# One maximum and one exponential over 768 keys in two attention stages

## The chip, the cores and the metric

The kernel runs on one core of a Trainium2 chip. Its time is the device time of one execution in microseconds (us). A core has TensorE (PE; its weight loads are shown as PEld), VectorE (DVE), ScalarE (ACT), GpSimd (POOL) and SyncE (SP); each works through its own queue of instructions, and they meet at semaphores. TensorE writes to PSUM, of which there are eight banks of 512 float32 columns for each of 128 partitions.

## The reference

The kernel computes a whole network on 512 tokens in float32: a first block (feed-forward, RWKV-7 time mix beside dilated attention, feed-forward), then two hybrid layers over the 512 tokens and 256 context tokens. Only the attention of the two hybrid layers matters here. Each layer has six heads of multi-head latent attention (mla, 96 channels for the scores) and six query heads of grouped-query attention (gqa, 64 channels):

```python
def block_attention(q, k, v):
    scale = D ** -0.5
    def one_block(qi):                       # 128 queries
        s = jnp.einsum('bqgrd,bkgd->bgrqk', qi, k).astype(jnp.float32) * scale
        p = jax.nn.softmax(s, axis=-1).astype(v.dtype)
        return jnp.einsum('bgrqk,bkgv->bqgrv', p, v)
...
    o_mla = block_attention(q_mla, jnp.concatenate([k_mla, k_mla_c], axis=1),
                            jnp.concatenate([v_mla, v_mla_c], axis=1))
...
    if last:
        return x_new, ctx
    oc_mla = block_attention(mla_query(pc, mla_q_norm, mla_w_uq, None, None), k_mla_c, v_mla_c)
```

A block of token queries looks at all 768 keys (512 tokens and 256 context). In the first of the two layers the two blocks of context queries look at the 256 context keys alone; the second layer has no such blocks.

## The kernel before

The program is a chain of stages: feed-forward, time mix, dilated attention, feed-forward, then for each hybrid layer a norm, input products, gates, small products, the heads, and the output product. Weights stream in through two slots: SyncE loads a block, ScalarE rounds it, GpSimd forms the remainder, TensorE multiplies. In the heads stages there is nearly no such traffic.

The heads stage of a layer is a loop over pairs `j`. A pair is one block of 128 queries for two heads at once (`a` = 0 and 1, called units `u = 2j + a`). For three groups of heads the loop goes through the query blocks of mla and then of gqa: four wide pairs (768 keys) and, in the first layer, two narrow ones (256 keys) each. A pair goes through these steps:

- TensorE, `scores(j)`: query times keys into `SCORES[a]`, which is a pair of neighbouring PSUM banks for each unit; columns 0 to 511 are the token keys (the part `l`), 512 to 767 the context keys (the part `h`). For mla (L2387) a unit has one matmul over 512 and one over 256 columns, unit 0 first. For gqa (L2393) there are three of 256 columns, and the two units alternate. In the records of the profile each float32 matmul stands twice.
- VectorE, `largest(u)`: the maximum along the keys (L2497), part by part as the scores come, and the scaling of the larger one to a bias (L2500; L2502 for narrow pairs).
- ScalarE, `exponent(u)`: the exponential (L2463) of each part from PSUM to `PX`, with its sum along the keys, which is read out by an instruction of its own behind each.
- TensorE, `turned(j)`: 128x128 transposes of the exponentials (L2410), four for the part `l` and two for `h`.
- ScalarE copies the turned part `l` out of PSUM (L2478), VectorE the part `h` (L2516). VectorE also adds the sums of the two parts (L2507) and inverts them (L2510).
- TensorE, `values(j)`: the inverse sums spread over partitions (L2421) and the products with the values (L2425).
- VectorE, `result(j)`: two multiplications with the gate and the inverse sum (L2522, L2524); ScalarE and VectorE split the result in two for the next product (L2468, L2527).

The order on each engine is written out. TensorE goes `turned(j)`, `scores(j + 1)`, `values(j)`. VectorE takes the maxima and scalings of pair `j`, then the result of pair `j - 1`, then the copies and the inverse of pair `j`. ScalarE takes the exponentials of pair `j`, its copies, then the rounding of pair `j - 1`. There is one set of `SCORES`, so the scores of the next pair can only be written behind the exponentials of this one, which the transposes ahead of them on TensorE ensure. The function `heads_steps` lists the names that the engines count on their semaphores, in that order.

Of the kernel before, what the change touches and what calls it, by code (L numbers as in the profile page):

```python
# [26 lines left out]
ACT = mybir.ActivationFunctionType  # L27
ALU = mybir.AluOpType
AX = mybir.AxisListType.X
# [3 lines left out]
T = 512  # L33
TC = 256
TT = T + TC
# [22 lines left out]
BLOCKS = T // P  # L58
# [11 lines left out]
KB = TT // P  # L70
# [171 lines left out]
def block_kernel(nc, xT, ctxT, vec, square, first, levels, trig, lora, wstream, outT):  # L242
    nblocks = wstream.shape[0]
    with ExitStack() as ctx:
# [1582 lines left out]
        class Layer:  # L1827
# [81 lines left out]
            def heads_steps(self):  # L1909
                us = self.units()  # L1910
                n = len(us) // 2
                pe, act, dve = [], [], []
                def scored(j):
                    parts = ("l", "h") if us[2 * j][3] < BLOCKS else ("h",)
                    if us[2 * j][0] == "gqa":
                        return [f"sc{z}{2 * j + a}" for z in parts for a in range(2)]
                    return [f"sc{z}{2 * j + a}" for a in range(2) for z in parts]
                pe += scored(0) + [f"v{b}" for b in range(KB)]
                act += ["v0", "v1"]
                for j in range(n):  # L1920
                    low = us[2 * j][3] < BLOCKS
                    parts = ("l", "h") if low else ("h",)
                    both = (2 * j, 2 * j + 1)
                    pe += [f"tr{z}{u}" for u in both for z in parts] + (scored(j + 1) if j + 1 < n else []) + [f"pv{j}"]
                    act += [f"ex{z}{u}" for u in both for z in parts] + ([f"pt{u}" for u in both] if low else [])
                    act += [f"hi{j - 1}"] if j else []
                    for u in both:
                        dve += [f"mx{z}{u}" for z in parts] + [f"nm{u}"]
                    dve += [f"rg{j - 1}", f"y{j - 1}"] if j else [f"v{b}" for b in range(2, KB)]
                    dve += [f"pt{2 * j}"] + ([f"lo{j - 2}"] if j > 1 else []) + ([f"dn{j}"] if low else []) + [f"ri{j}", f"pt{2 * j + 1}"]  # L1930
                j = n - 1
                return pe, act + [f"hi{j}"], dve + [f"lo{j - 1}", f"rg{j}", f"y{j}", f"lo{j}"]

# [425 lines left out]
        def scale_of(kind):  # L2359
            return (MLA_NOPE + MLA_ROPE if kind == "mla" else HD) ** -0.5  # L2360

        COLS = 2 * KB
        SCORES, TURNED = two_banks[0:2], two_banks[2:4]
        VALUES = two_banks[3][:, TT:TT + 2 * P]

        def part_cols(u):
            return slice(u % COLS, u % COLS + 1), slice(COLS + u % COLS, COLS + u % COLS + 1)

        value_bank = lambda b: bank[4 + (b + 2) % 4]
        def head_values_out(b):  # L2370
# [2 lines left out]
        def heads_tensor(pe, L):  # L2373
# [4 lines left out]
            def scores(j):  # L2378
                kind, i, _, qb = us[2 * j]
                low = qb < BLOCKS  # L2380
                qs = slice(qb * P, (qb + 1) * P)
                pe.sem_inc(tensor_ready)
                if kind == "mla":
                    for a in range(2):
                        for z, at, w in (("l", 0, T), ("h", T, TC)):
                            if low or at:
                                pe.matmul(SCORES[a][:, at:at + w], QAM[:, i * 2 + a, qs], KAM[:, i * 2 + a, at:at + w], start=True, stop=True)\  # L2387
                                  .then_inc(*S.inc(f"sc{z}{2 * j + a}"))
                else:
                    for at in range(0 if low else T, TT, TC):  # L2390
                        for a in range(2):
                            hs = slice(a * HD, a * HD + HD)
                            mm = pe.matmul(SCORES[a][:, at:at + TC], QAG[hs, i, qs], KAG[hs, at:at + TC], start=True, stop=True)  # L2393
                            if at + TC in (T, TT):
                                mm.then_inc(*S.inc(f"sc{'l' if at < T else 'h'}{2 * j + a}"))
            def turned(j):
                low = us[2 * j][3] < BLOCKS
                for a in range(2):
                    u = 2 * j + a
                    for z, bs in (("l", range(BLOCKS)), ("h", range(BLOCKS, KB))):  # L2400
                        if z == "l" and not low:
                            continue
                        pe.wait_ge(*A.at(f"ex{z}{u}"))
                        if j == 0:
                            pe.wait_ge(*V.at("v5" if a else "v3"))
                        if j and a and z == "h":
                            pe.wait_ge(*V.at(f"y{j - 1}"))
                        pe.sem_inc(tensor_ready)
                        for b in bs:
                            mm = pe.transpose(TURNED[a][:, b * P:(b + 1) * P], PX[:, a, b * P:(b + 1) * P], eye)  # L2410
                        mm.then_inc(*S.inc(f"tr{z}{u}"))
# [36 lines left out]
        def heads_scalar(act, L):  # L2448
            st = L.heads
            A, V, S = st.act, st.dve, st.pe  # L2450
            us = L.units()
            n = len(us) // 2
            for b in range(2):
                act.wait_ge(*S.at(f"v{b}"))
                act.activation(*head_values_out(b), ACT.Copy).then_inc(*A.inc(f"v{b}"))
            def exponent(u):
                kind, _, a, qb = us[u]
                act.wait_ge(*V.at(f"nm{u}"))
                if u >= 2:
                    act.wait_ge(*S.at(f"trh{u - 2}"))  # L2460
                for z, c, cols in (("l", slice(0, T), part_cols(u)[0]), ("h", slice(T, TT), part_cols(u)[1])):
                    if z == "h" or qb < BLOCKS:
                        act.activation(PX[:, a, c], SCORES[a][:, c], ACT.Exp, scale=scale_of(kind), bias=NM2[:, u % COLS:u % COLS + 1],  # L2463
                                       accum_out=DEN2[:, cols]).then_inc(*A.inc(f"ex{z}{u}"))
            def rounded_part(j):
                kind, i, _, qb = us[2 * j]
                act.wait_ge(*V.at(f"y{j}"))
                act.activation(YHI[:, i + (0 if kind == "mla" else MLA_HEADS // 2), qb * P:(qb + 1) * P], YQ[:, j % 2, :], ACT.Copy)\  # L2468
                   .then_inc(*A.inc(f"hi{j}"))
            for j in range(n):  # L2470
                for a in range(2):
                    exponent(2 * j + a)
                if us[2 * j][3] < BLOCKS:
                    for a in range(2):
                        act.wait_ge(*S.at(f"trl{2 * j + a}"))
                        if j:
                            act.wait_ge(*S.at(f"pv{j - 1}"))
                        act.activation(PTS[:, a, 0:T], TURNED[a][:, 0:T], ACT.Copy).then_inc(*A.inc(f"pt{2 * j + a}"))  # L2478
                if j:
                    rounded_part(j - 1)  # L2480
                else:
                    round_block(act, L.out.b0 + 1)
            rounded_part(n - 1)

        def heads_vector(dve, L):
# [3 lines left out]
            n = len(us) // 2  # L2489
            def largest(u):  # L2490
                kind, i, a, qb = us[u]
                lo, hi = part_cols(u)
                nm = NM2[:, u % COLS:u % COLS + 1]
                for z, c, cols in (("l", slice(0, T), lo), ("h", slice(T, TT), hi)):
                    if z == "h" or qb < BLOCKS:
                        dve.wait_ge(*S.at(f"sc{z}{u}"))
                        dve.tensor_reduce(MX2[:, cols], SCORES[a][:, c], AX, ALU.max).then_inc(*V.inc(f"mx{z}{u}"))  # L2497
                dve.wait_ge(*V.at(f"mxh{u}"))
                if qb < BLOCKS:
                    dve.tensor_scalar(nm, MX2[:, lo], MX2[:, hi], -scale_of(kind), ALU.max, ALU.mult).then_inc(*V.inc(f"nm{u}"))  # L2500
                else:
                    dve.tensor_scalar(nm, MX2[:, hi], -scale_of(kind), None, ALU.mult).then_inc(*V.inc(f"nm{u}"))  # L2502
            def inverse(j):
                c, h = 2 * j % COLS, COLS + 2 * j % COLS
                dve.wait_ge(*A.at(f"exh{2 * j + 1}"))
                if us[2 * j][3] < BLOCKS:
                    dve.tensor_tensor(DEN2[:, c:c + 2], DEN2[:, c:c + 2], DEN2[:, h:h + 2], ALU.add).then_inc(*V.inc(f"dn{j}"))  # L2507
                    dve.wait_ge(*V.at(f"dn{j}"))
                    h = c
                dve.reciprocal(DEN2[:, c:c + 2], DEN2[:, h:h + 2]).then_inc(*V.inc(f"ri{j}"))  # L2510
            def high_part(u):
                j, a = u // 2, u % 2
                dve.wait_ge(*S.at(f"trh{u}"))
# [446 lines left out]
```

## Time and profile before

| | us |
|---|---|
| median of three runs (lowest, highest) | 2551.69 (2548.96, 2557.23) |
| span of the profiled execution, first to last instruction | 2548.6 |
| TensorE busy | 2434.8 (96%) |
| VectorE busy | 1208.9 (47%) |
| ScalarE busy | 1074.7 (42%) |
| GpSimd busy | 891.9 (35%) |

The page gives no time for the profiled execution other than its span. A matmul's end is modelled, so a busy TensorE need not be one at its peak. Shares over the whole span say little about a stage: the two heads stages lie at 1914 to 2090 us and 2351 to 2490 us. Useful views for them are the busy times in a window, the chain of waits in order of time, and the timeline of one pair.

### The profile page before, as it was taken

What the parts mean: (1) busy time and instruction counts of PE and PEld (TensorE: products, weight loads), DVE (VectorE), ACT (ScalarE), POOL (GpSimd) and SP (SyncE); (2) the same over time, 40 slices, a digit from 0 to 9 for tenths busy, and PEclk for the clock granted to TensorE, in tenths of its full rate; (3) what the DMA queues carried; (4) which work ended last, traced back from release to release, by engine and by line L of the source; (5) the groups of instructions that cost most, each with busy time, mean ns of one, the idle gap of its engine ahead of it and who ended that gap; (6) DMA issues with size and microseconds to landing.
All of it is one profiled execution on the core that took longest, in us unless ns stands there. A gap on an engine that the chain in (4) does not pass through costs nothing. (4 is left out here: it accounts for less than half of the span.)

```text
span 2548.6 us, 48956 instructions
## 1 busy us (share of the span) xinstructions
PE 2434.8 (96%) x18458; PEld 1982.8 (78%) x18458; DVE 1208.9 (47%) x2008; ACT 1074.7 (42%) x2172; POOL 891.9 (35%) x678
## 2 busy tenths in 40 slices
PE   8999999999999999999999999989999999898998
PEld 6888887878787887787888888878876678776776
DVE  3222225435363637454232222136777773567774
ACT  4333234444443434564343332243346652435662
POOL 3444453333334244224544444522320003233003
PEclk9999999999999999999999999989999999999999
DMA  4333332222223232112432333321110002122002
GB/s 145 97 92 99 102 107 93 68 91 62 91 66 93 60 98 75 59 50 77 140 101 91 99 99 99 100 65 50 58 50 26 2 1 66 42 74 76 17 2 75
DMA packets 52293, 188.44 MB, mean 74 GB/s; under 512 B 5792, under 2 KB 6048, under 8 KB 52000
## 3 DMA queue, kind: packets, MB, share of 16 engines
q1 hardware_dynamic: 50976, 181.74, 23.2%
q10 hardware_dynamic: 1152, 4.26, 0.5%
q8 instruction: 133, 2.18, 0.3%
q14 instruction: 32, 0.26, 0.0%
HBM read 183.88 MB, written 2.10 MB: 73 GB/s over the span
## 5 line engine op out<-in xcount | busy, mean ns | idle before, releaser
L2676 POOL TENSOR_TENSOR WLO<-RAW,WHI 128x512 fp32r<-128x512 f32 x668 | 886.1, 1348 | 1629.2 <-ACT WHI L318 1629.2
L318 ACT ACTIVATE WHI<-RAW 128x512 fp32r<-128x512 f32 x672 | 386.8, 623 | 972.1 <-PE psum L334 756.4
L332 PE MATMUL psum<-HHI,WHI 128*128 128x512 f32 x848 | 335.0, 395 | 14.1 <-POOL WLO L2671 8.7
L334 PE MATMUL psum<-HHI,WLO 128*128 128x512 f32 x848 | 331.1, 390 | 0.0
L333 PE MATMUL psum<-HLO,WHI 128*128 128x512 f32 x848 | 330.9, 390 | 0.0
L332 PE MATMUL psum<-H2HI,WHI 128*128 128x512 f32 (+1 forms) x536 | 196.8, 367 | 12.2 <-DVE H2LO L442 7.6
L332 PEld LDWEIGHTS psum<-HHI,WHI 128*128 128x128 f32 x848 | 159.8, 188 | 50.8 <-POOL WLO L2671 8.7
L333 PE MATMUL psum<-H2LO,WHI 128*128 128x512 f32 (+1 forms) x536 | 189.1, 353 | 0.0
L334 PE MATMUL psum<-H2HI,WLO 128*128 128x512 f32 (+1 forms) x536 | 188.9, 352 | 0.0
L333 PEld LDWEIGHTS psum<-HLO,WHI 128*128 128x128 f32 x848 | 159.9, 189 | 33.7 <-issue 1.2
L334 PEld LDWEIGHTS psum<-HHI,WLO 128*128 128x128 f32 x848 | 159.7, 188 | 33.6
L2463 ACT ACTIVATE PX<-psum,NM 128x512 f32<-128x512 f32 (+1 forms) x216 | 121.0, 565 | 93.6 <-DVE NM L2500 80.3
L332 PE MATMUL psum<-GHI,WHI 128*128 128x512 f32 x352 | 137.0, 389 | 0.9 <-DVE psum L666 0.9
L334 PE MATMUL psum<-GHI,WLO 128*128 128x512 f32 x352 | 136.9, 389 | 0.0
L333 PE MATMUL psum<-GLO,WHI 128*128 128x512 f32 x352 | 136.9, 389 | 0.0
L332 PEld LDWEIGHTS psum<-H2HI,WHI 128*128 128x128 f32 x536 | 102.6, 191 | 32.3 <-issue 8.2
L666 DVE TENSOR_TENSOR psum<-psum,FRSTD 128x512 f32<-128x512 f32 x44 | 30.8, 699 | 189.7 <-PE psum L334 189.6
L2497 DVE TENSOR_REDUCE MX<-psum 128x1 f32<-128x512 f32 (+1 forms) x216 | 108.0, 537 | 23.7 <-PE psum L2393 15.9
L333 PEld LDWEIGHTS psum<-H2LO,WHI 128*128 128x128 f32 x536 | 102.5, 191 | 16.2 <-issue 2.7
L334 PEld LDWEIGHTS psum<-H2HI,WLO 128*128 128x128 f32 x536 | 102.3, 191 | 14.0
L2410 PE MATMUL psum<-SQC,PX 128*128 128x128 f32 x624 | 89.0, 280 | 21.4 <-ACT PX L2463 14.4
L2410 PEld LDWEIGHTS psum<-SQC,PX 128*128 128x128 f32 x624 | 65.5, 141 | 43.4 <-issue 41.5
(416 smaller groups left out, 4835.5 us busy)
## 6 DMA issues: line engine op xcount, KB each, us to landing
RAW<-in_wstream SPq DMA_DIRECT2D x335, 512.0 KB, 3.6
X<-in_xT SPq DMA_DIRECT2D x8, 256.0 KB, 6.9
W3S<-in_lora ACTq DMA_DIRECT2D x5, 384.0 KB, 3.2
out_T<-OUT SPq DMA_DIRECT2D x3, 512.0 KB, 2.7
XC<-in_ctxT ACTq DMA_DIRECT2D x1, 1024.0 KB, 4.9
TRIG<-in_trig ACTq DMA_DIRECT2D x1, 960.0 KB, 8.0
FCC<-in_first SPq DMA_DIRECT2D x1, 576.0 KB, 8.7
RAW<-in_wstream SPq DMA_DIRECT2D x2, 256.0 KB, 3.8
```

The source lines that it names most:

```text
L318: act.activation(WHI[:, q % 2, half], RAW[:, q % 2, half], ACT.Copy).then_inc(rounded, 1)
L332: pe.matmul(out, tile_of(WHI, slot, u), hi(kt), start=first and last[0], stop=False)
L333: pe.matmul(out, tile_of(WHI, slot, u), lo(kt), start=False, stop=False)
L334: mm = pe.matmul(out, tile_of(WLO, slot, u), hi(kt), start=False, stop=end and last[1])
L666: dve.tensor_tensor(up, up, FRSTD[:, :], ALU.mult).then_inc(*st.dve.inc(f"up{n}"))
L2410: mm = pe.transpose(TURNED[a][:, b * P:(b + 1) * P], PX[:, a, b * P:(b + 1) * P], eye)
L2463: act.activation(PX[:, a, c], SCORES[a][:, c], ACT.Exp, scale=scale_of(kind), bias=NM2[:, u % COLS:u % COLS + 1], accum_out=DEN2[:, cols]) ...
L2497: dve.tensor_reduce(MX2[:, cols], SCORES[a][:, c], AX, ALU.max).then_inc(*V.inc(f"mx{z}{u}"))
L2676: pool.tensor_tensor(WLO[:, s, half], RAW[:, s, half], WHI[:, s, half].bitcast(F32), ALU.subtract).then_inc(split, 1)
```

## The change

A wide unit gets one maximum over its 768 columns and one exponential with one sum. TensorE signals `sc{u}` only when both parts of a unit's scores are written; VectorE waits for that, and the scaling has one operand to take from memory where it had two. The transposes of a unit wait for its one exponential. The addition of two partial sums is no longer there, and the small buffers of maxima and sums use one column for each unit, in a ring of 24 where it was 12. Narrow pairs keep their instructions.

```diff
-                        for z, at, w in (("l", 0, T), ("h", T, TC)):
+                        for at, w in ((0, T), (T, TC)):
                             if low or at:
-                                pe.matmul(SCORES[a][:, at:at + w], QAM[:, i * 2 + a, qs], KAM[:, i * 2 + a, at:at + w], start=True, stop=True)\
-                                  .then_inc(*S.inc(f"sc{z}{2 * j + a}"))
+                                mm = pe.matmul(SCORES[a][:, at:at + w], QAM[:, i * 2 + a, qs], KAM[:, i * 2 + a, at:at + w], start=True, stop=True)
+                        mm.then_inc(*S.inc(f"sc{2 * j + a}"))
...
-                            if at + TC in (T, TT):
-                                mm.then_inc(*S.inc(f"sc{'l' if at < T else 'h'}{2 * j + a}"))
+                            if at + TC == TT:
+                                mm.then_inc(*S.inc(f"sc{2 * j + a}"))
...
-                        pe.wait_ge(*A.at(f"ex{z}{u}"))
+                        if z == "l" or not low:
+                            pe.wait_ge(*A.at(f"ex{u}"))
...
-                for z, c, cols in (("l", slice(0, T), part_cols(u)[0]), ("h", slice(T, TT), part_cols(u)[1])):
-                    if z == "h" or qb < BLOCKS:
-                        act.activation(PX[:, a, c], SCORES[a][:, c], ACT.Exp, scale=scale_of(kind), bias=NM2[:, u % COLS:u % COLS + 1],
-                                       accum_out=DEN2[:, cols]).then_inc(*A.inc(f"ex{z}{u}"))
+                c = keys_at(qb)
+                act.activation(PX[:, a, c], SCORES[a][:, c], ACT.Exp, scale=scale_of(kind), bias=NM2[:, unit_col(u)],
+                               accum_out=DEN2[:, unit_col(u)]).then_inc(*A.inc(f"ex{u}"))
...
-                for z, c, cols in (("l", slice(0, T), lo), ("h", slice(T, TT), hi)):
-                    if z == "h" or qb < BLOCKS:
-                        dve.wait_ge(*S.at(f"sc{z}{u}"))
-                        dve.tensor_reduce(MX2[:, cols], SCORES[a][:, c], AX, ALU.max).then_inc(*V.inc(f"mx{z}{u}"))
-                dve.wait_ge(*V.at(f"mxh{u}"))
-                if qb < BLOCKS:
-                    dve.tensor_scalar(nm, MX2[:, lo], MX2[:, hi], -scale_of(kind), ALU.max, ALU.mult).then_inc(*V.inc(f"nm{u}"))
-                else:
-                    dve.tensor_scalar(nm, MX2[:, hi], -scale_of(kind), None, ALU.mult).then_inc(*V.inc(f"nm{u}"))
+                dve.wait_ge(*S.at(f"sc{u}"))
+                dve.tensor_reduce(MX2[:, unit_col(u)], SCORES[a][:, keys_at(qb)], AX, ALU.max).then_inc(*V.inc(f"mx{u}"))
+                dve.wait_ge(*V.at(f"mx{u}"))
+                dve.tensor_scalar(NM2[:, unit_col(u)], MX2[:, unit_col(u)], -scale_of(kind), None, ALU.mult).then_inc(*V.inc(f"nm{u}"))
...
-                if us[2 * j][3] < BLOCKS:
-                    dve.tensor_tensor(DEN2[:, c:c + 2], DEN2[:, c:c + 2], DEN2[:, h:h + 2], ALU.add).then_inc(*V.inc(f"dn{j}"))
-                    dve.wait_ge(*V.at(f"dn{j}"))
-                    h = c
-                dve.reciprocal(DEN2[:, c:c + 2], DEN2[:, h:h + 2]).then_inc(*V.inc(f"ri{j}"))
+                dve.reciprocal(DEN2[:, c:c + 2], DEN2[:, c:c + 2]).then_inc(*V.inc(f"ri{j}"))
```

On TensorE this is a wide gqa pair of the first hybrid layer before the change: the transposes of unit 0 and of unit 1, and the scores of the next pair behind them (`PX` holds the exponentials, `SQC` the identity).

```order
L2410 MATMUL psum<-SQC,PX 128x128 [waits scalar_steps]
L2410 MATMUL psum<-SQC,PX 128x128 x3
L2410 MATMUL psum<-SQC,PX 128x128 [waits scalar_steps]
L2410 MATMUL psum<-SQC,PX 128x128
L2410 MATMUL psum<-SQC,PX 128x128 [waits scalar_steps]
L2410 MATMUL psum<-SQC,PX 128x128 x3
L2410 MATMUL psum<-SQC,PX 128x128 [waits scalar_steps,vector_steps]
L2410 MATMUL psum<-SQC,PX 128x128
L2393 MATMUL psum<-KAG,QAG 128x256 x6
```

The same place after the change:

```order
L2408 MATMUL psum<-SQC,PX 128x128 [waits scalar_steps]
L2408 MATMUL psum<-SQC,PX 128x128 x5
L2408 MATMUL psum<-SQC,PX 128x128 [waits scalar_steps]
L2408 MATMUL psum<-SQC,PX 128x128 x3
L2408 MATMUL psum<-SQC,PX 128x128 [waits vector_steps]
L2408 MATMUL psum<-SQC,PX 128x128
L2390 MATMUL psum<-KAG,QAG 128x256 x6
```

TensorE waited for ScalarE four times and now waits twice, each time ahead of a unit's first transpose; number and order of its matmuls are as before.

On VectorE, the maxima (`MX_65`) and scalings (`NM_66`) of one wide pair, the previous pair's result and the inverse of the sums (`DEN_67`), before the change:

```order
L2497 TENSOR_REDUCE MX_65<-psum 128x1 [waits tensor_steps] x2
L2500 TENSOR_SCALAR NM_66<-MX_65 128x1 [waits vector_steps]
L2497 TENSOR_REDUCE MX_65<-psum 128x1 [waits tensor_steps] x2
L2500 TENSOR_SCALAR NM_66<-MX_65 128x1 [waits vector_steps]
L2522 TENSOR_TENSOR RG<-psum,GATES 128x128 [waits tensor_steps]
L2524 TENSOR_TENSOR YQ<-psum,RG 128x128 [waits vector_steps]
L2516 COPY PTS<-psum 128x256 [waits tensor_steps]
L2527 TENSOR_TENSOR YLO<-YQ,YHI 128x128 [waits scalar_steps]
L2507 TENSOR_TENSOR DEN_67<-DEN_67 128x2 [waits scalar_steps]
L2510 RECIPROCAL DEN_67<-DEN_67 128x2 [waits vector_steps]
```

And after it:

```order
L2490 TENSOR_REDUCE MX_65<-psum 128x1 [waits tensor_steps]
L2492 TENSOR_SCALAR NM_66<-MX_65 128x1 [waits vector_steps]
L2490 TENSOR_REDUCE MX_65<-psum 128x1 [waits tensor_steps]
L2492 TENSOR_SCALAR NM_66<-MX_65 128x1 [waits vector_steps]
L2508 TENSOR_TENSOR RG<-psum,GATES 128x128 [waits tensor_steps]
L2510 TENSOR_TENSOR YQ<-psum,RG 128x128 [waits vector_steps]
L2502 COPY PTS<-psum 128x256 [waits tensor_steps]
L2513 TENSOR_TENSOR YLO<-YQ,YHI 128x128 [waits scalar_steps]
L2496 RECIPROCAL DEN_67<-DEN_67 128x2 [waits scalar_steps]
```

Two maxima and the addition (L2507) are gone; the inverse waits for ScalarE itself.

## Rows read from the trace of the kernel before

**Rows 1.** Busy us (instructions) in the heads stages; then PEclk, DMA share, GB/s

```profile
core 0: us, PE busy (x) PEld busy (x) DVE busy (x) ACT busy (x) POOL busy (x), PEclk, DMA share, GB/s
1914.48:2090.18 175.70, 160.05 (x1458) 117.84 (x1458) 136.95 (x437) 110.12 (x331) 5.28 (x4) 1.00 0.03 7
2351.57:2489.84 138.27, 131.14 (x1219) 99.58 (x1219) 105.19 (x316) 93.71 (x271) 5.02 (x4) 1.00 0.04 13
```

**Rows 2.** Chain of waits, second heads stage: start us, us, what

```profile
2371.66 2.58 PE psum L2387 x8
...
2374.61 1.31 PE psum L2425 x24
2375.92 1.46 PE psum L2410 x12
2377.38 1.11 PE psum L2393 x8
2378.49 1.01 DVE MX L2497 x2
```

**Rows 3.** Timeline, a gqa pair: start us, us, engine, instructions [idle before, releaser]

```profile
1962.89 1.57 PE L2393 MATMUL psum<-KAG,QAG 64*128 64x256 f32 x12
...
1964.05 1.02 DVE L2497 TENSOR_REDUCE MX<-psum 128x1 f32<-128x512 f32 x2 [0.63 <-PE psum L2393]
...
1965.11 0.21 DVE L2500 TENSOR_SCALAR NM<-MX 128x1 f32<-128x1 f32 x1
1965.24 1.01 DVE L2497 TENSOR_REDUCE MX<-psum 128x1 f32<-128x512 f32 x2
1965.36 0.69 ACT L2463 ACTIVATE PX<-psum,NM 128x512 f32<-128x512 f32 x1 [1.78 <-DVE NM L2500]
...
1966.54 0.69 ACT L2463 ACTIVATE PX<-psum,NM 128x512 f32<-128x512 f32 x1
...
1967.46 0.86 PE L2410 MATMUL psum<-SQC,PX 128*128 128x128 f32 x6 [0.32 <-ACT PX L2463]
...
1968.25 0.70 PE L2393 MATMUL psum<-KAG,QAG 64*128 64x256 f32 x4
```

**Rows 4.** Timeline, an mla pair

```profile
2365.78 2.75 PE L2387 MATMUL psum<-KAM,QAM 128*128 128x512 f32 x8
...
2366.84 1.02 DVE L2497 TENSOR_REDUCE MX<-psum 128x1 f32<-128x512 f32 x2 [0.44 <-PE psum L2387]
...
2368.13 1.02 DVE L2497 TENSOR_REDUCE MX<-psum 128x1 f32<-128x512 f32 x2
...
2370.13 1.53 PE L2410 MATMUL psum<-SQC,PX 128*128 128x128 f32 x12
...
2371.50 2.75 PE L2387 MATMUL psum<-KAM,QAM 128*128 128x512 f32 x8
```

**Rows 5.** Groups by form, whole trace: xcount, busy us, mean ns, idle before

```profile
L2463 ACT ACTIVATE PX<-psum,NM 128x512 f32<-128x512 f32 x96 | 65.9, 687 | 81.6 <-DVE NM L2500 80.3
L2463 ACT ACTIVATE PX<-psum,NM 128x256 f32<-128x256 f32 x120 | 56.0, 467 | 12.0 <-DVE NM L2502 12.0
L2387 PE MATMUL psum<-KAM,QAM 128*128 128x512 f32 x96 | 49.2, 594 | 0.6 <-PE psum L334 0.6
L2310 ACT ACTIVATE YHI<-YC 128x768 fp32r<-128x768 f32 x2 | 1.7, 846 | 5.9 <-DVE YC L2346 5.9
L1706 DVE TENSOR_REDUCE MX<-psum 128x3 f32<-128x768 f32 x4 | 3.8, 948 | 0.0
```

**Rows 6.** One line's instructions: duration ns min/median/max, first and last start

```profile
L2502 DVE TENSOR_SCALAR NM<-MX x24: 153/154/154, 1941.3 to 2087.4; 128x1 f32<-128x1 f32 x24
```

**Rows 7.** Timeline, an mla pair that follows a narrow gqa pair

```profile
1976.98 1.02 DVE L2497 TENSOR_REDUCE MX<-psum 128x1 f32<-128x512 f32 x2
...
1979.21 0.86 PE L2410 MATMUL psum<-SQC,PX 128*128 128x128 f32 x6 [0.22 <-ACT PX L2463]
```

**Rows 8.** Timeline, the first pair of the first heads stage

```profile
1918.92 1.28 ACT L2463 ACT_TABLE_LOAD   x1
...
1922.26 0.87 PE L2410 MATMUL psum<-SQC,PX 128*128 128x128 f32 x6 [0.26 <-ACT PX L2463]
```

More of the change, by code:

```diff
@@ L1913, in scored @@
                 def scored(j):
[L1914 to L1917, printed above, removed]
+                    return [f"sc{2 * j + a}" for a in range(2)]
                 pe += scored(0) + [f"v{b}" for b in range(KB)]
@@ L1924, in heads_steps @@
                     pe += [f"tr{z}{u}" for u in both for z in parts] + (scored(j + 1) if j + 1 < n else []) + [f"pv{j}"]
-                    act += [f"ex{z}{u}" for u in both for z in parts] + ([f"pt{u}" for u in both] if low else [])
+                    act += [f"ex{u}" for u in both] + ([f"pt{u}" for u in both] if low else [])
                     act += [f"hi{j - 1}"] if j else []
                     for u in both:
-                        dve += [f"mx{z}{u}" for z in parts] + [f"nm{u}"]
+                        dve += [f"mx{u}", f"nm{u}"]
                     dve += [f"rg{j - 1}", f"y{j - 1}"] if j else [f"v{b}" for b in range(2, KB)]
-                    dve += [f"pt{2 * j}"] + ([f"lo{j - 2}"] if j > 1 else []) + ([f"dn{j}"] if low else []) + [f"ri{j}", f"pt{2 * j + 1}"]
+                    dve += [f"pt{2 * j}"] + ([f"lo{j - 2}"] if j > 1 else []) + [f"ri{j}", f"pt{2 * j + 1}"]
                 j = n - 1
@@ L2360, in scale_of @@
             return (MLA_NOPE + MLA_ROPE if kind == "mla" else HD) ** -0.5
-        COLS = 2 * KB
+        COLS = 4 * KB
         SCORES, TURNED = two_banks[0:2], two_banks[2:4]
         VALUES = two_banks[3][:, TT:TT + 2 * P]
-        def part_cols(u):
-            return slice(u % COLS, u % COLS + 1), slice(COLS + u % COLS, COLS + u % COLS + 1)
+        unit_col = lambda u: slice(u % COLS, u % COLS + 1)
+        keys_at = lambda qb: slice(0 if qb < BLOCKS else T, TT)
         value_bank = lambda b: bank[4 + (b + 2) % 4]
@@ L2491, in largest @@
                 kind, i, a, qb = us[u]
-                lo, hi = part_cols(u)
-                nm = NM2[:, u % COLS:u % COLS + 1]
-                for z, c, cols in (("l", slice(0, T), lo), ("h", slice(T, TT), hi)):
-                    if z == "h" or qb < BLOCKS:
-                        dve.wait_ge(*S.at(f"sc{z}{u}"))
-                        dve.tensor_reduce(MX2[:, cols], SCORES[a][:, c], AX, ALU.max).then_inc(*V.inc(f"mx{z}{u}"))
-                dve.wait_ge(*V.at(f"mxh{u}"))
-                if qb < BLOCKS:
-                    dve.tensor_scalar(nm, MX2[:, lo], MX2[:, hi], -scale_of(kind), ALU.max, ALU.mult).then_inc(*V.inc(f"nm{u}"))
-                else:
-                    dve.tensor_scalar(nm, MX2[:, hi], -scale_of(kind), None, ALU.mult).then_inc(*V.inc(f"nm{u}"))
-            def inverse(j):
-                c, h = 2 * j % COLS, COLS + 2 * j % COLS
-                dve.wait_ge(*A.at(f"exh{2 * j + 1}"))
-                if us[2 * j][3] < BLOCKS:
-                    dve.tensor_tensor(DEN2[:, c:c + 2], DEN2[:, c:c + 2], DEN2[:, h:h + 2], ALU.add).then_inc(*V.inc(f"dn{j}"))
-                    dve.wait_ge(*V.at(f"dn{j}"))
-                    h = c
-                dve.reciprocal(DEN2[:, c:c + 2], DEN2[:, h:h + 2]).then_inc(*V.inc(f"ri{j}"))
+                dve.wait_ge(*S.at(f"sc{u}"))
+                dve.tensor_reduce(MX2[:, unit_col(u)], SCORES[a][:, keys_at(qb)], AX, ALU.max).then_inc(*V.inc(f"mx{u}"))
+                dve.wait_ge(*V.at(f"mx{u}"))
+                dve.tensor_scalar(NM2[:, unit_col(u)], MX2[:, unit_col(u)], -scale_of(kind), None, ALU.mult).then_inc(*V.inc(f"nm{u}"))
+            def inverse(j):
+                c = 2 * j % COLS
+                dve.wait_ge(*A.at(f"ex{2 * j + 1}"))
+                dve.reciprocal(DEN2[:, c:c + 2], DEN2[:, c:c + 2]).then_inc(*V.inc(f"ri{j}"))
             def high_part(u):
```

## Prediction

> **What bounds the kernel now.** I first looked at where the change lives: the two stretches in which the attention heads run, 1914 to 2090 us and 2351 to 2490 us, 314 us together [rows 1]. In both TensorE is busy over 90% of the time and its granted clock is 1.00 throughout, while VectorE is busy 76 to 78% and ScalarE 63 to 68%. So nothing is simply full, and the next view is the chain of waits. It shows two regimes side by side [rows 2]. Up to 2377.38 it is TensorE alone: scores 2.58, values 1.31, transposes 1.46 us, one after the other. These are mla pairs. From 2377.38 it leaves TensorE: scores, then VectorE's two maxima (1.01 us), its scaling, ScalarE's exponential, and back to TensorE for six transposes (0.86 [rows 3]). These are gqa pairs. So the same four steps are hidden in one kind of pair and are the path in the other.
>
> The timeline gives both periods, counted from the first score matmul of a pair to that of the next: 5.37 us for gqa (1962.89 to 1968.25 [rows 3]) and 5.72 for mla (2365.78 to 2371.50 [rows 4]). Only pairs over all 768 keys are touched. Counts from the grouped rows [rows 5]: 96 matmul records of form 128x512 on the mla score line at four to a pair make 24 mla pairs, and the 96 exponentials over 512 at two to a pair make 48 wide pairs, so 24 are gqa. The 12 narrow pairs (256 keys) keep one maximum and one exponential, as they had.
>
> **One gqa pair, step by step.** [rows 3]
>
> 1. The maximum waits longer. Before, it starts once the first 512 columns of scores are there, 1.17 us after the scores begin (1962.89 to 1964.05). Now it waits for all 768. In mla, 1536 columns take 2.58 us [rows 2], so 256 columns cost 0.43. In gqa the twelve records take 1.57 us in all and the chain puts 1.11 on the eight ahead of the maximum [rows 2, 3]: 0.46 for the rest. I take 0.43, the rest of the difference being the modelled end of the last matmul: **+0.43**.
> 2. Maximum and scaling of the first unit. The two maxima take 1.01 us end to end. One maximum over 128x768 in the same memory appears elsewhere in this trace and takes 948 ns [rows 5]. The scaling with two pointer operands takes 0.21 and becomes the form with one, 0.15, which the narrow pairs already use [rows 6]. From start of the maximum to start of the exponential that is 1.31 before and 0.95 + 0.04 + 0.15 + 0.03 = 1.17 after, the 0.04 and 0.03 being the gaps that stand there now: **-0.14**.
> 3. From the first exponential to the second: 1.18 now (1965.36 to 1966.54), in which ScalarE runs without a pause. Afterwards ScalarE would be free after 0.90, but VectorE's second maximum starts 0.13 after the first scaling starts (1965.11 to 1965.24) and takes 0.95 + 0.04 + 0.15 + 0.03 more, so the second exponential follows the first by 0.13 + 1.17 - 0.15 - 0.03 = 1.12: **-0.06**. ScalarE's larger saving is not used: VectorE comes last.
> 4. From the second exponential to its transposes: now 0.92 (1966.54 to 1967.46), because TensorE turns the first 512 columns while ScalarE still works on the other 256. Then all six transposes wait for the whole row. An exponential over 512 takes 687 ns and over 256 takes 467 [rows 5], so 256 columns cost 220 and one over 768 about 907 (an estimate from these two rows): **+0.22**. The six transposes then take what they take now (0.79 to the next scores), since they already run back to back after the first part.
>
> Sum +0.45 us, a period of 5.82. Nothing covers it: the scores of the next pair stand behind these transposes on TensorE, and the maxima stand behind the scores. Times 24: **10.8 us**.
>
> **One mla pair.** [rows 4] Here TensorE's own work has to be overtaken before anything costs. With the same steps, the first maximum moves from 2366.84 to 2367.27. The second starts at 2368.13 now, on its scores; it moves to 2368.56, its exponential to 2368.56 + 0.95 + 0.04 + 0.15 + 0.03 = 2369.73, and its transposes become ready 0.92 + 0.22 later, at 2370.87. TensorE gets to them at 2370.13 plus half of the 1.46 us that twelve transposes take [rows 2], 2370.86. So the cover is used up almost exactly: 0 to 0.1. I take +0.10, since a wait that ends last leaves a small gap on TensorE. In 20 mla pairs: **2.0 us**. In two more, which follow a narrow gqa pair, TensorE has little to do in front: transposes start at 1979.21 now [rows 7]. The second maximum moves from 1976.98 to 1977.41, the transposes to 1977.41 + 1.17 + 1.14 = 1979.72: +0.5 each, **1.0 us**. In the first pair of each stretch a table load of 1.28 us ends at 1920.20, ahead of the first exponential, and the maxima have long been done [rows 8]; 1920.22 + 0.90 + 1.14 = 1922.26 is the time at which the second unit's transposes start now. Nothing.
>
> **Edits at nothing.** 48 additions of the two halves of the sum go, off the path: VectorE makes them after the second exponential while TensorE turns and scores. The wider column buffers cost no instruction. TensorE's and the DMA queues' instructions stay the same in number; no transfer is moved. Behind the longer wait of the maximum stand the scaling and the previous pair's result, whose inputs come later than that anyway. Behind the longer wait of the transposes stand the next scores, which is the cost counted above.
>
> **Sum.** 10.8 + 2.0 + 1.0 = 13.8 us on a span of 2548.6, the only time that the profile gives of its own execution. The three timed runs have a median of 2551.69 (2548.96 to 2557.23), 3.1 above that span, and I add to the median: **2565.5 us**, 0.54% slower.
>
> Bounds of what the trace does not show. The exponential over two banks at once: not under 0.85 (ScalarE's copy of 128x768 out of SBUF, 846 ns [rows 5]) and not over 687 + 467 = 1.15; that is -0.06 to +0.25 in every pair on the path, -1.4 to +11. I take 0.91, next to the lower end. The maximum over 768 into one column: 0.95 as the row has it, at most the 1.01 that two take now: up to +0.13 a pair, 6 us. The extra wait: 0 (the next 256 columns were there whenever the maximum started) to 0.46.
>
> The pages speak for the other sign. The Trainium skill, "Advanced Engine Details and Errata", section TRN2 Errata, The Read-Write Bubble, says that ScalarE and VectorE pay a memory latency between instructions and not inside one, advises large tiles, and says that one instruction may read several PSUM banks. The rows agree with the fixed part (467 - 220 = 247 ns of each exponential do not depend on its width). By that rule alone the merge is a gain, which is the third case below.
>
> **Rivals.**
>
> - *The mla pairs lose too.* For it: their cover is used up to within 0.1 us [rows 4], so any instruction longer than estimated is paid in all 22. With the merged exponential at 1.05 and the maximum at 1.0, each gqa pair pays 2 x 0.05 + 0.14 = 0.24 more and each mla pair, whose first maximum is not on the path, 0.19 more: 24 x 0.24 + 22 x 0.19 = 10 us more, 2575.5 us.
> - *The wait for the last 256 columns costs nothing.* If the score matmuls had all ended by the time the maximum starts, item 1 falls away and the gqa sum is +0.02, while the mla pairs stay covered: 2552 us, no change. Against it: in rows 3 the maximum starts at 1964.05 and the last score records run to 1964.46.
> - *The fixed costs decide (faster).* If ScalarE's queue sets the gqa period, each unit gives back 1.18 - 0.90 = 0.28 us, two units a pair, 24 pairs: 13.4 us, 2538 us. For it: ScalarE goes from the first unit's exponentials to the second's without a pause. It decides from the point at which the second scaling is done before ScalarE is free. Against it: VectorE needs 1.12 us a unit (item 3) where ScalarE will need 0.90, and the rule leaves out both the wait of item 1 and the overlap of item 4, which are not instructions.
>
> **How the numbers follow.** My forecast 0.62, its own range 2559 to 2573 (gqa between +0.3 and +0.65, mla between 0 and 0.2); mla loses too 0.18; wait costs nothing 0.14; fixed costs 0.06. A measurement of this kernel tells some 0.3% (7.7 us) from no change. Slower by more than that: 0.62 x 0.97 + 0.18 = 0.78; within: 0.16; faster: 0.06. The range for 8 in 10 leaves out the fast case and the outer part of the others: 2554 to 2577.
>
> **What would show it.** In the changed profile: the gap ahead of the maxima in a gqa pair grows from 0.63 to about 1.05 us; its period goes from 5.37 to about 5.8, with the six transposes of the second unit behind the end of the exponential; the maximum near 0.95 us and the exponential near 0.91; mla periods stay between 5.72 and 5.9; the granted clock stays 1.00 in both stretches. The prediction is wrong if gqa periods stay at 5.4 or fall, or if the merged instructions take as long as the two parts did.

## The result, and the profile after

The changed kernel takes a median of 2567.1 us (2557.69 to 2570.81, nine runs) against 2553.52 (2548.96 to 2557.49, nine runs) of the kernel before on the same chips: a ratio of 1.0049, 95% interval 1.0040 to 1.0059, or 12.5 us (10 to 15) slower; the two medians lie 13.6 us apart. The forecast was 13.8 us slower, 2565.5 us. One execution further below, of the kernel with the change in mla pairs alone, took 3063.62 us at a granted clock of 0.747; it is left out of that kernel's median and ratio.

The two heads stages answer to [rows 1]: busy us of each engine and number of instructions in each stretch, then the granted clock, DMA share and GB/s, in the changed kernel.

```profile
core 0: us, PE busy (x) PEld busy (x) DVE busy (x) ACT busy (x) POOL busy (x), PEclk, DMA share, GB/s
1918.82:2100.55 181.73, 160.21 (x1458) 118.22 (x1458) 126.82 (x365) 100.91 (x235) 5.29 (x4) 1.00 0.02 7
2365.21:2508.62 143.41, 131.36 (x1218) 99.95 (x1218) 95.13 (x244) 84.29 (x175) 5.01 (x4) 1.00 0.04 12
```

They take 325.1 us where they took 314.0: 11.2 us longer. VectorE and ScalarE are each busy some 20 us less in them, so the change does what it says, and TensorE does as much as before in a longer time. The timeline of a gqa pair shows where it waits; it answers to [rows 3].

```profile
1968.49 1.57 PE L2390 MATMUL psum<-KAG,QAG 64*128 64x256 f32 x12
...
1970.09 0.96 DVE L2490 TENSOR_REDUCE MX<-psum 128x1 f32<-128x768 f32 x1 [1.06 <-PE psum L2390]
...
1971.09 0.15 DVE L2492 TENSOR_SCALAR NM<-MX 128x1 f32<-128x1 f32 x1
1971.15 0.95 DVE L2490 TENSOR_REDUCE MX<-psum 128x1 f32<-128x768 f32 x1
1971.27 0.90 ACT L2460 ACTIVATE PX<-psum,NM 128x768 f32<-128x768 f32 x1 [2.09 <-DVE NM L2492]
...
1972.33 0.90 ACT L2460 ACTIVATE PX<-psum,NM 128x768 f32<-128x768 f32 x1
...
1973.46 0.84 PE L2408 MATMUL psum<-SQC,PX 128*128 128x128 f32 x6 [0.21 <-ACT PX L2460]
...
1974.23 0.49 PE L2390 MATMUL psum<-KAG,QAG 64*128 64x256 f32 x2
```

The period, scores to scores, is 5.74 us where it was 5.37. VectorE waits 1.06 us ahead of the maximum where it waited 0.63, and the six transposes of the second unit start 1.13 us behind its exponential where they started 0.92. The merged instructions, as groups by form (to [rows 5]; count, busy us and mean ns, then idle time before them):

```profile
L2490 DVE TENSOR_REDUCE MX<-psum 128x1 f32<-128x768 f32 x96 | 91.7, 955 | 47.6 <-PE psum L2390 25.5 <-PE psum L2384 18.9
L2460 ACT ACTIVATE PX<-psum,NM 128x768 f32<-128x768 f32 x96 | 86.5, 901 | 102.5 <-DVE NM L2492 101.0
```

The maximum takes 955 ns and the exponential 901, where 948 and 907 were expected. An mla pair, to [rows 4]:

```profile
2379.42 2.75 PE L2384 MATMUL psum<-KAM,QAM 128*128 128x512 f32 x8
...
2380.92 0.96 DVE L2490 TENSOR_REDUCE MX<-psum 128x1 f32<-128x768 f32 x1 [0.87 <-PE psum L2384]
...
2382.21 0.96 DVE L2490 TENSOR_REDUCE MX<-psum 128x1 f32<-128x768 f32 x1
...
2383.39 0.91 ACT L2460 ACTIVATE PX<-psum,NM 128x768 f32<-128x768 f32 x1 [0.30 <-DVE NM L2492]
...
2383.78 1.59 PE L2408 MATMUL psum<-SQC,PX 128*128 128x128 f32 x12
...
2385.21 0.60 PE L2384 MATMUL psum<-KAM,QAM 128*128 128x512 f32 x1
```

In the kernel before, the second unit's exponential of the pair in [rows 4] was:

```profile
2369.44 0.69 ACT L2463 ACTIVATE PX<-psum,NM 128x512 f32<-128x512 f32 x1
```

Counted from the first score matmul, the maxima come 0.44 us later (1.50 and 2.79 where it was 1.06 and 2.35) and the second exponential 0.31 us later (3.97 where it was 3.66). And yet the period is 5.78 to 5.79 where it was 5.72: the twelve transposes start when they did and take 1.59 us instead of 1.53, the small gap in their middle being what is left of the wait.

The span of this profile is 18.5 us longer, of which only 11.2 lie in the heads stages. The other 7.3 became a question for the experiments.

### The profile page after: what moved, and what is told of

Its sections match the earlier page's. It is cut to its first block and busy times, and to the rows that moved or that the text cites. A ratio compares the mean times of both kernels' runs of the same rounds, so it can differ in the third digit from the quotient of the medians.

```text
span 2567.1 us, 48620 instructions
## 1 busy us (share of the span) xinstructions
PE 2443.6 (95%) x18458; PEld 1991.7 (78%) x18458; DVE 1189.0 (46%) x1864; ACT 1056.4 (41%) x1980; POOL 891.4 (35%) x678
## 5 line engine op out<-in xcount | busy, mean ns | idle before, releaser
L332 PE MATMUL psum<-HHI,WHI 128*128 128x512 f32 x848 | 335.1, 395 | 13.8 <-POOL WLO L2657 9.8
L332 PE MATMUL psum<-H2HI,WHI 128*128 128x512 f32 (+1 forms) x536 | 200.0, 373 | 11.2 <-DVE H2LO L442 6.6
L2460 ACT ACTIVATE PX<-psum,NM 128x768 f32<-128x768 f32 (+1 forms) x120 | 97.8, 816 | 114.4 <-DVE NM L2492 112.9
L2490 DVE TENSOR_REDUCE MX<-psum 128x1 f32<-128x768 f32 (+1 forms) x120 | 101.8, 848 | 48.9 <-PE psum L2390 26.7
```

Of the source, the lines that this page charges most:

```text
L332: pe.matmul(out, tile_of(WHI, slot, u), hi(kt), start=first and last[0], stop=False)
L2490: dve.tensor_reduce(MX2[:, unit_col(u)], SCORES[a][:, keys_at(qb)], AX, ALU.max).then_inc(*V.inc(f"mx{u}"))
```

## The experiments

In what was expected of each run, quoted here, theory A is the prediction's: the maximum waits for the last 256 columns, the transposes for the whole exponential. Theory B lays the loss to the exponential alone. For the trace, a period is the time from the first score matmul of a pair to that of the next, and "the heads" are the two stretches from the first score matmul to the output product, 313.97 us in the kernel before.

Most kernels are the one before with two rules, which say for a wide unit (kind, group, 0 or 1, query block) whether it gets one maximum and one exponential:

```diff
+                parts = (("l", slice(0, T), lo), ("h", slice(T, TT), hi))
+                if qb < BLOCKS and ONE_MAX(us[u]):
+                    parts = (("h", slice(0, TT), hi),)
...
+                parts = (("l", slice(0, T), part_cols(u)[0]), ("h", slice(T, TT), part_cols(u)[1]))
+                if qb < BLOCKS and ONE_EXP(us[u]):
+                    parts = (("h", slice(0, TT), part_cols(u)[0]),)
...
-                        pe.wait_ge(*A.at(f"ex{z}{u}"))
+                        if not (low and z == "h" and ONE_EXP(us[u])):
+                            pe.wait_ge(*A.at(f"ex{'h' if ONE_EXP(us[u]) else z}{u}"))
```

**The maximum alone.**

```diff
+ONE_MAX = lambda unit: True
+ONE_EXP = lambda unit: False
```

> One maximum over 768 keys, the exponential still in two parts. Theory A (the gqa pair pays for a longer wait, and apart from that for the transposes that start behind the whole exponential): the first maximum of a gqa pair starts 0.43 us later and is 0.12 us shorter with its scaling, the second exponential follows the first after 1.18 us (ScalarE's two parts, not VectorE), transposes 0.92 us behind it: period 5.37 + 0.31 = 5.68. mla stays at 5.72 (second exponential 0.29 later, transposes ready at 2370.65 of the old trace, TensorE there at 2370.86). 24 x 0.31 + 2 x 0.3 = 8 us slower. Theory B (the loss is the exponential's alone, the wait for the scores is paid back by the shorter maximum): gqa 5.37, no change in time.

Measured: 2559.28 against 2552.73 us, ratio 1.0028 (1.0017 to 1.0040); heads 320.65, 6.7 longer. gqa period 5.62, mla 5.72, and 5.59 for the two mla pairs behind narrow gqa pairs. Theory B falls. A's 5.68 was 0.06 too long, and the timeline of the gqa pair says why:

```profile
1954.70 0.69 ACT L2472 ACTIVATE PX<-psum,NM 128x512 f32<-128x512 f32 x1 [2.09 <-DVE NM L2514]
...
1955.57 0.15 DVE L2514 TENSOR_SCALAR NM<-MX 128x1 f32<-128x1 f32 x1
...
1955.83 0.68 ACT L2472 ACTIVATE PX<-psum,NM 128x512 f32<-128x512 f32 x1
```

ScalarE's second unit starts 1.13 us behind the first and its bias has been ready for 0.1 us. So ScalarE needs 1.12 to 1.13 us for the two parts, and the 1.18 of the kernel before [rows 3] held a short wait for VectorE.

**The exponential alone.**

```diff
+ONE_MAX = lambda unit: False
+ONE_EXP = lambda unit: True
```

> One exponential over 768 keys, the maximum still in two parts. Theory A: the second exponential starts when it did (VectorE's second scaling ends at the same time as ScalarE's first two parts did), its transposes 1.13 us behind it where it was 0.92, then 0.02 us less: gqa period 5.37 + 0.19 = 5.56, mla 5.72: 24 x 0.19 + 2 x 0.2 = 5 us slower. Theory B: gqa 5.74 as with both edits, 9 us slower.

Measured: 2558.7 against 2552.73 us, ratio 1.0023 (1.0014 to 1.0032); heads 318.86, 4.9 longer. gqa 5.56, mla 5.72, behind narrow pairs 5.47 to 5.48: A to the hundredth, and B falls. In the gqa pair ScalarE now stops ahead of the second unit, for VectorE:

```profile
1959.62 0.90 ACT L2472 ACTIVATE PX<-psum,NM 128x768 f32<-128x768 f32 x1 [0.19 <-DVE NM L2512]
...
1960.76 0.85 PE L2416 MATMUL psum<-SQC,PX 128*128 128x128 f32 x6 [0.33 <-ACT PX L2472]
```

**The wait alone.**

```diff
-                        dve.wait_ge(*S.at(f"sc{z}{u}"))
+                        dve.wait_ge(*S.at(f"sch{u}"))
```

> The kernel before, in which the first part of each wide maximum waits for all 768 columns of scores; all instructions as before. Theory A: gqa period 5.37 + 0.43 = 5.80, mla 5.72 to 5.75, the two mla pairs behind narrow gqa pairs 5.28 + 0.43: 24 x 0.43 + 2 x 0.43 = 11 us slower, as much as the whole change costs in the two stretches. Theory B: gqa 5.37, no change.

Measured: 2565.89 against 2552.73 us, ratio 1.0057 (1.0044 to 1.0069). gqa 5.80 (+0.43), mla 5.72, behind narrow pairs 5.71. In a gqa pair the idle time ahead of the maximum is as long as in the changed kernel, 1.06 us:

```profile
1952.76 1.57 PE L2393 MATMUL psum<-KAG,QAG 64*128 64x256 f32 x12
...
1954.35 1.02 DVE L2497 TENSOR_REDUCE MX<-psum 128x1 f32<-128x512 f32 x2 [1.06 <-PE psum L2393]
...
1958.55 0.49 PE L2393 MATMUL psum<-KAG,QAG 64*128 64x256 f32 x2
```

The heads take 326.77 us, 12.8 longer, of which 1.6 are one fall of the clock that the last part of this section comes to; without it 11.2. With all instructions as before, this one wait costs as much as the whole change. In a gqa pair, what the merged instructions save and the lost overlap of the transposes nearly cancel each other (+0.43 for the wait alone, +0.37 for the whole change).

**The two kinds of pairs.**

```diff
+ONE_MAX = ONE_EXP = lambda unit: unit[0] == "gqa"
...
+ONE_MAX = ONE_EXP = lambda unit: unit[0] == "mla"
```

(The rules stand as two lines in each of the two kernels.)

> The whole change in gqa pairs alone. Theory A: gqa 5.74, mla 5.72, the two mla pairs behind narrow ones 5.28: 24 x 0.37 = 9 us slower. If mla pairs pay more than their period shows, less.

> The whole change in mla pairs alone. Theory A: TensorE's own work covers the longer chain but for 0.06 us: mla 5.78, the two behind narrow gqa pairs 5.78 where they were 5.28, gqa 5.37: 20 x 0.06 + 2 x 0.5 = 2.3 us slower. Rival (no cover, each wide mla pair pays as a gqa pair does): 22 x 0.4 = 9 us.

Measured: gqa alone 2564.74 against 2553.19 us, ratio 1.0038 (1.0025 to 1.0051), heads 322.97, 9.0 longer, periods 5.74, 5.72 and 5.28. mla alone 2556.06, ratio 1.0009 (0.9998 to 1.0019), heads 316.09, 2.1 longer, periods 5.37, 5.78 and 5.78. 9.0 and 2.1 make 11.1, where the whole change costs 11.2. The second time can't be told from no change; its periods can. The rival without cover falls. The heads as windows, to [rows 1], first with gqa pairs changed, then with mla pairs changed:

```profile
1918.89:2099.09 180.20, 159.65 (x1458) 118.26 (x1458) 130.78 (x401) 106.30 (x283) 5.29 (x4) 1.00 0.02 7
2363.71:2506.48 142.77, 130.70 (x1219) 100.00 (x1219) 99.00 (x280) 89.92 (x223) 5.03 (x4) 1.00 0.04 12
```

```profile
1915.17:2092.36 177.19, 160.65 (x1459) 117.75 (x1459) 132.63 (x401) 104.73 (x283) 5.29 (x4) 1.00 0.02 7
2353.66:2492.56 138.90, 131.81 (x1218) 99.45 (x1218) 101.02 (x280) 88.14 (x223) 5.03 (x4) 1.00 0.04 13
```

**Who sets the second exponential.** Two more kernels, each for one profile, with the rules in gqa pairs alone:

```diff
+ONE_MAX = lambda unit: unit[0] == "gqa" and unit[2] == 1
+ONE_EXP = lambda unit: False
...
+ONE_MAX = lambda unit: False
+ONE_EXP = lambda unit: unit[0] == "gqa" and unit[2] == 0
```

> In wide gqa pairs, unit 1 alone gets one maximum; every exponential stays in two parts, mla as before. Theory A (VectorE's second scaling, not ScalarE, sets the start of the second exponential in the kernel before): it ends 0.12 us earlier, ScalarE's two parts of unit 0 then take over at 1.12 us, as they do behind the table load of the first pair: gqa period 5.37 - 0.06 = 5.31. Theory B' (ScalarE sets it already): 5.37.

> In wide gqa pairs, unit 0 alone gets one exponential; every maximum stays in two parts, mla as before. Theory A: ScalarE is free 0.2 us earlier and waits for VectorE: gqa period 5.37. Theory B': 5.37 - 0.2 = 5.17. For the stretch between the two heads stages: 265.8 us if it follows the gqa period (theory F, below), since that is unchanged.

Measured: gqa periods 5.31 and 5.36 to 5.37, as A had them; theory B' falls in both. A shorter second maximum gains 0.06 and then meets ScalarE, which takes 1.13 us from unit 0 to unit 1; a shorter first exponential gains nothing and meets VectorE. A line or two from each:

```profile
1952.55 0.69 ACT L2472 ACTIVATE PX<-psum,NM 128x512 f32<-128x512 f32 x1 [2.57 <-DVE NM L2512]
...
1953.68 0.69 ACT L2472 ACTIVATE PX<-psum,NM 128x512 f32<-128x512 f32 x1
```

```profile
1955.79 0.69 ACT L2472 ACTIVATE PX<-psum,NM 128x512 f32<-128x512 f32 x1 [0.18 <-DVE NM L2512]
```

The two engines were within 0.06 us of each other in the kernel before. (Times of these two kernels: 2555.14 and 2550.89 us, one execution each, the kernel before at 2549.4; too few to tell 1 us.)

**A version that takes both.**

```diff
+ONE_MAX = lambda unit: unit[0] == "gqa" and unit[2] == 1
+ONE_EXP = lambda unit: unit[0] == "gqa" and unit[2] == 0
```

> Wide gqa pairs only, each unit with what the path wants of it: unit 0 keeps its maximum in two parts (it may start on the first 512 columns) and has one exponential; unit 1 has one maximum (its scores have long been there) and keeps its exponential in two parts (its transposes start behind the first). mla as before. Theory A: the second exponential waits for VectorE, whose second maximum with its scaling is 0.12 us shorter, and ScalarE is free 0.9 after the first: gqa period 5.37 - 0.12 = 5.25, mla 5.72; 24 x 0.12 = 3 us faster, at the edge of what times can tell. Theory B' (what a merged instruction saves on the path is ScalarE's): 5.37 - 0.2 or less, as ScalarE's 0.2 of unit 0 is what counts.

Measured: 2550.64 against 2553.19 us, ratio 0.9991 (0.9981 to 1.0000), heads 310.94, 3.0 shorter, gqa 5.24 (A had 5.25), mla 5.72. It beats the changed kernel clearly. Against the kernel before the gain is in the trace (all 24 gqa pairs 0.13 us shorter), while the times only just allow it.

```profile
1953.04 1.02 DVE L2509 TENSOR_REDUCE MX<-psum 128x1 f32<-128x512 f32 x2 [0.63 <-PE psum L2398]
...
1954.22 0.95 DVE L2509 TENSOR_REDUCE MX<-psum 128x1 f32<-128x768 f32 x1
1954.34 0.90 ACT L2472 ACTIVATE PX<-psum,NM 128x768 f32<-128x768 f32 x1 [1.78 <-DVE NM L2512]
...
1955.39 0.69 ACT L2472 ACTIVATE PX<-psum,NM 128x512 f32<-128x512 f32 x1
```

Maximum in two parts where the path waits for scores, in one where they lie ready; exponential in one where only ScalarE's time counts, in two where TensorE waits. The second exponential follows the first after 1.05 us.

**The 7 us outside the heads.** Unchanged kernels, for their traces: the changed one twice more, the one before twice more.

> The changed kernel once more. In its first profile the two heads stretches became 11 us longer and the rest of the program 7 us. Theory C (the rest is TensorE's clock, which falls to its lower level in other places and more often or less often from one execution to the next, whatever the change): gqa 5.74, mla 5.79 again, but the time outside the heads differs by several us from that of the first profile, and the stretches at the lower clock lie elsewhere. Theory D (the change itself shifts later stages into a slower course): the same 7 us again.

> The kernel before once more, for its trace alone. Theory C (clock outside the heads is chance): heads periods to the hundredth as before, the time outside the heads some us off that of the first profile. Theory E (the falls of the clock inside gqa pairs, seen in two of the runs with a longer wait, come with any kernel): such a fall may show here too; if it needs the longer wait, none.

> The kernel before a third time, for the stretch from the last narrow pair of the first heads stage to the first pair of the second one. It took 265.8 us in the three profiles whose gqa period was 5.37, and 267.4 to 269.2 in the seven whose period was longer or shorter, all of it in stretches in which TensorE's clock is at its lower level. Theory F (the length of the heads stage places those stretches, so this comes with the change): 265.8 again. Theory C (chance from one execution to the next): it may be 267 to 269.

> The changed kernel a third time, for the same stretch: 269 (theory F; it was 269.2 and 269.0), or anything from 265.8 to 269 (theory C). gqa 5.74, mla 5.78. A fall of the clock inside a gqa pair, as in one of its two profiles so far, may or may not show.

Measured: span less heads is 2234.6, 2231.6 and 2238.4 us in the three profiles of the kernel before and 2241.9, 2237.1 and 2233.3 in those of the changed one. The ranges overlap and D falls. The first profiles say as much by themselves: of the 7.3 us, 4.3 lie ahead of the first heads stage (it starts at 1918.82 us where it started at 1914.48), where the two programs are the same and nothing that was changed has run yet. Over the six profiles that part takes 1910.83 to 1918.82 us, and by the profile's clock records 20.5 us of it are at the lower clock in the shortest and 44.4 in the longest. The stretch between the heads stages, last narrow pair to first wide one, took 269.02 us in the third profile of the kernel before and 267.93 in that of the changed one, so F falls too. It goes with the clock, as two profiles of the kernel before show (windows: length, busy times, granted clock), the first from the first profile, the second from the third:

```profile
2085.68:2351.57 265.89, 242.88 (x1177) 196.68 (x1177) 157.10 (x205) 99.50 (x175) 85.44 (x62) 0.97 0.20 60
```

```profile
2086.68:2355.70 269.02, 246.94 (x1177) 200.21 (x1176) 157.01 (x205) 99.48 (x175) 85.90 (x62) 0.94 0.19 59
```

The same 1177 matmul records, a granted clock of 0.97 and 0.94, 3.1 us. The repeat of the changed kernel, at 2565.87 against 2552.73 us, has the ratio 1.0052 (1.0038 to 1.0065).

In two of the changed kernel's three profiles, and in that of the wait alone, the clock also falls once inside a heads stage, always in the first gqa pair of a group, behind a narrow mla pair. Here in the third profile of the changed kernel, TensorE's timeline and the pairs as windows:

```profile
2004.19 0.61 PE L2423 MATMUL psum<-PTS,VAM 128*64 128x128 f32 x8
2006.34 0.85 PE L2408 MATMUL psum<-SQC,PX 128*128 128x128 f32 x6 [1.54 <-ACT PX L2460]
2007.39 1.35 PE L2408 MATMUL psum<-SQC,PX 128*128 128x128 f32 x6 [0.20 <-ACT PX L2460]
```

```profile
2002.42:2008.66 6.24, 4.49 (x37) 3.32 (x36) 3.85 (x12) 2.79 (x6) 0.00 (x0) 0.91 0.00 0
2008.66:2015.54 6.88, 6.00 (x53) 4.66 (x53) 3.74 (x10) 3.06 (x8) 0.00 (x0) 0.83 0.01 4
2015.54:2021.28 5.74, 4.87 (x53) 3.85 (x52) 3.74 (x10) 3.27 (x8) 0.00 (x0) 1.00 0.01 3
```

Before it fell TensorE had sat idle for 1.54 us, since the pair in front is narrow and its values are few. The two pairs take 0.5 and 1.1 us more. Expectation E (any kernel) is not borne out: none of the nine profiles with a gqa period of 5.62 or less has such a fall, three of the five with 5.74 or 5.80 do. Each profile has three such places, gqa pairs behind a narrow mla pair: with 1.45 to 1.54 us of idle time a fall came at 3 of 15 of them, with 1.02 to 1.33 us at none of 27. That is few, and the gqa-only kernel with the same idle time of 1.54 us has none, so that the longer wait causes them is likely, not shown.

## Why the prediction was right

*The path.* Two regimes, as forecast: gqa pairs pay nearly all (9.0 us of 11.2), mla pairs keep TensorE as their bound. The forecast's 10.8 + 2.0 + 1.0 measured 9.0 + 1.2 + 1.0, the first of these by the heads with gqa pairs alone (24 periods at +0.37 make 8.9), the second from 20 periods at +0.06, the third from two at +0.50; the first pair of a stage cost nothing (8.41 where it was 8.45).

*Item 1, the wait*: +0.43 forecast, and 0.43 measured twice, by the gap ahead of the maximum (1.06 less 0.63) and by the wait alone. *Item 2*: -0.14 forecast, start to start 1.18 where it was 1.31, so -0.13. *Item 4*: +0.22 forecast, 1.13 less 0.92, so +0.21, and 0.02 less behind it.

*Item 3 was mis-sized*: -0.06 forecast, -0.12 measured (1.06 where it was 1.18). I let VectorE's second maximum start 0.13 us behind the first scaling, as it does with the long form of the scaling; behind the short form it starts 0.06 behind it (1971.09 to 1971.15). It keeps its place to the end of the scaling (0.08 us ahead of it before, 0.09 now), not to its start. That, over 24 pairs, is 1.4 of the 1.8 us by which the forecast's 10.8 was too much. The words "ScalarE runs without a pause" were wrong as well: of its 1.18 us, 0.06 were a wait for VectorE. That VectorE comes last was right all the same.

*The rivals.* The mla pairs' cover held, with 0.06 us paid. The wait for the scores was not free. The fixed costs did fall: 687 + 467 - 901 leaves 253 ns saved in each exponential. Of these the path got some 0.07 us, through item 3: with the maximum alone ScalarE's two parts held the second exponential at 1.13 us behind the first, with both edits it is VectorE that comes last, at 1.06. The Trainium skill, "Advanced Engine Details and Errata" (TRN2 Errata, The Read-Write Bubble), says that on ScalarE and VectorE a memory latency shows between instructions and is hidden inside one; the 253 ns agree with it.

*What the sum left out.* 11.2 us in the heads and 12.5 (10 to 15) in the times agree. The forecast's 13.8 came nearer to the times than its parts deserve: the clock inside the heads, 1.6 us in two of three profiles, was not in it. Of the signs that were named, one failed: the granted clock stayed at 1.00 in both stretches in the first profile alone, and was 0.99 in the first stretch in the other two.

## What to carry to other kernels

Two instructions in a chain over several engines are also two chances for the next engine to start: merging saves the fixed cost once for each instruction, and costs the head start of whoever waited for the first part. Count each by the place on the path: here one wait of 0.43 us outweighed all that the merged instructions saved. And merge unit by unit, in the pairs that are the path: where the inputs lie ready and nobody waits for the first half, one instruction is better; where either fails, two.

## What the runs had in store besides

Two executions of one kernel differ by some us in stages that no change touched, by where TensorE's clock is at its lower level: the same 1177 matmul records took 265.8 to 269.0 us in three profiles of the kernel before. Of the 7 us outside the changed stages in a first profile, more than half lay ahead of the first instruction that was changed; periods of single pairs, where the clock does not fall, repeat to 0.01 us and tell differences that the times of whole executions do not.
